# Eight landing places, smaller retrieval parts in front, and half blocks and a third lane in the mixer

## What is computed

```python
def peer_ffn(x, wq, sub_keys, u, v):
    ...
    def chunk(xc):
        q = (xc @ wq).reshape(PEER_CHUNK, PEER_HEADS, 2, half)
        sc = jnp.einsum('chpd,hpnd->chpn', q, sub_keys, preferred_element_type=jnp.float32)
        s1, i1 = lax.top_k(sc[:, :, 0], PEER_TOPK)
        s2, i2 = lax.top_k(sc[:, :, 1], PEER_TOPK)
        ...
        top_s, pos = lax.top_k(cand, PEER_TOPK)
        eidx = jnp.take_along_axis(cidx, pos, axis=-1)
        g = jax.nn.softmax(top_s, axis=-1)
        u_sel = jnp.take(u, eidx, axis=0)
        a = jax.nn.gelu(jnp.einsum('chkd,cd->chk', u_sel, xc, ...), approximate=False)
        w = (g * a).astype(x.dtype)
        v_sel = jnp.take(v, eidx, axis=0)
        return jnp.einsum('chk,chkd->cd', w, v_sel)
...
def second_block(x, c, ctx, c_ctx, w_mod, ...):
        sh1, sc1, g1, sh2, sc2, g2 = [m[:, None, :] for m in _modulation(c, w_mod[i], b_mod[i], 6)]
        cm = _modulation(c_ctx, w_mod[i], b_mod[i], 2 if last else 6)
        hc = _rmsnorm(ctx, norm_mix_pre[i]) * (1.0 + cm[1]) + cm[0]
        sf_c = _state_features(hc, w_in[i], gdn_conv[i], gdn_a_log[i], gdn_dt_bias[i])
        init = _recurrent_mixers(sf_c, None, None, zero_state, ret_log_decay[i])
        ...
        ret_x, gdn_x, _ = _recurrent_mixers(sf_x, _apply_rope(rq, cos, sin), gq, init, ret_log_decay[i])
        x = x + g1 * _rmsnorm(_mixer_out(ret_x, gdn_x, rg, gz, gates, *out_p), norm_mix_post[i])
        h2 = _rmsnorm(x, norm_ffn_pre[i]) * (1.0 + sc2) + sh2
        x = x + g2 * _rmsnorm(_moe(h2, *moe_p), norm_ffn_post[i])
```

## Time and profile before

| | us |
|---|---|
| median of 3 runs (lowest to highest) | 3165.72 (3165.24 to 3170.95) |
| the profiled execution | 3162.61 |
| its span | 3160.8 |
| up to the first gather of layer 0 | 225.5 |
| layer 0, first gather to last sum | 831.9 |
| attention and front of layer 1 | 209.6 |
| layer 1, first gather to last sum | 707.9 |
| mixer, to 2527 | 552 |
| experts, 2527 to the end | 633.8 |

### The profile page before, as it was taken

One profiled execution on the slowest core, in us unless ns is written; L12 is line 12 of the kernel. 1 busy time (PEld: TensorE's weight loads), 2 busy tenths in 40 slices (PEclk: granted clock), 3 DMA queues, 4 the chain that ended last, 5 costly groups with the idle time before them and its releaser, 6 DMA issues.

```text
span 3160.8 us, 29029 instructions
## 1 busy us (share of the span) xinstructions
PE 2464.3 (78%) x9500; PEld 1296.6 (41%) x9500; DVE 1600.1 (51%) x3286; ACT 842.7 (27%) x2277; POOL 830.3 (26%) x718
## 2 busy tenths in 40 slices
PE   7898778878979889888877777868787667667673
PEld 4683334424545467433322222546553432222221
DVE  5554737679777555564758544364533422111112
ACT  1312343443433131233333333322110211111110
POOL 1002323335545210333434433012100012122221
PEclk9799988998989989999999999889998778888786
DMA  6039988897979702999999999210113199999992
GB/s 261 1 125 411 369 345 309 329 385 270 379 285 382 299 27 81 377 412 411 420 421 402 421 421 381 107 40 32 49 54 150 46 408 395 396 384 390 375 380 79
DMA packets 128913, 885.91 MB, mean 280 GB/s; under 512 B 23024, under 2 KB 23408, under 8 KB 31600
## 3 DMA queue, kind: packets, MB, share of 16 engines
q0 software_dynamic: 86976, 553.74, 44.5%
q1 hardware_dynamic: 41776, 330.22, 26.0%
HBM read 877.56 MB, written 37.75 MB: 290 GB/s over the span
## 4 chain that ended last, share of the span: by engine, by line
PE 44%; DMA 24%; DVE 19%; ACT 6%; issue 4%; POOL 2%; SPq 1%; DVEq 0%; POOLq 0%; ACTq 0%
PE ps L155 42%; DMA ring<-in_peer_uv,idx_u 10%; DMA ring<-in_w_gu 5%; DVE ring L1278 5%; ACT arena L125 4%; DVE arena L76 4%; DMA ring<-in_w_down 3%; DMA arena<-in_w_gu 2%; PE ps L158 2%; DVE ring L76 1%; DMA arena<-in_peer_uv,idx_u 1%; DVE iu L113 1%; DVE arena L1278 1%; ACT L125 1%; DVE arena L109 1%
## 5 line engine op out<-in xcount | busy, mean ns | idle before, releaser
L155 PE MATMUL ps<-ring,arena 128*128 128x512 f32 (+3 forms) x3200 | 1234.0, 647 | 305.0 <-ACT arena L125 182.2
L155 PEld LDWEIGHTS ps<-ring,arena 128*128 128x128 f32 (+2 forms) x3200 | 457.9, 180 | 980.8 <-issue 593.7
L1278 DVE CUSTOM_DVE_ANT_0 ring<-ring,h 128x1024 f32<-128x1024 f32 x428 | 538.9, 1259 | 396.0 <-DMA ring<-in_peer_uv,idx_u 368.2
L2335 POOL DMA_INDIRECT ring<-in_peer_uv,idx_u x428 | 466.0, 1089 | 794.2 <-PE ps L155 662.2
L155 PE MATMUL ps<-arena 128*128 128x128 f32 (+7 forms) x2184 | 501.2, 417 | 156.4 <-ACT arena L125 88.6
L125 ACT ACTIVATE arena<-arena 128x1 f32<-128x1 f32 (+3 forms) x1089 | 291.7, 268 | 840.3 <-DVE arena L1278 751.2
L155 PEld LDWEIGHTS ps<-arena 128*128 128x128 f32 (+3 forms) x2184 | 286.2, 197 | 334.4 <-issue 151.1
L155 PE MATMUL ps<-ring,hT 128*128 128x512 f32 (+1 forms) x704 | 323.1, 615 | 44.7 <-DMA ring<-in_w_in 13.1
L76 DVE TENSOR_TENSOR arena<-arena,ps 128x512 f32<-128x512 f32 (+1 forms) x134 | 77.1, 576 | 445.0 <-ACT arena L125 352.9
L125 ACT ACTIVATE arena<-ps 128x512 f32<-128x512 f32 (+5 forms) x182 | 100.3, 551 | 745.6 <-PE ps L155 671.2
L125 ACT ACTIVATE arena<-cst,arena 128x128 f32<-128x128 f32 x512 | 205.5, 401 | 175.1 <-PE ps L155 135.3
(11 more groups left out here) (117 smaller groups left out, 1633.2 us busy)
## 6 DMA issues: line engine op xcount, KB each, us to landing
ring<-in_w_gu SPq DMA_DIRECT2D x98, 1024.0 KB, 29.4
ring<-in_w_down SPq DMA_DIRECT2D x52, 1024.0 KB, 28.1
ring<-in_w_in SPq DMA_DIRECT2D x22, 2048.0 KB, 9.4
arena<-in_w_gu SPq DMA_DIRECT2D x30, 1024.0 KB, 30.4
ring<-in_w_mod SPq DMA_DIRECT2D x12, 2048.0 KB, 11.2
ring<-in_peer_wq SPq DMA_DIRECT2D x8, 2048.0 KB, 7.9
ring<-in_w_o SPq DMA_DIRECT2D x6, 2048.0 KB, 15.9
arena<-in_w_down SPq DMA_DIRECT2D x12, 1024.0 KB, 25.0
```

Source lines behind the costliest of these rows:

```text
L155: return self.e.matmul(o, lhsT, rhs, start=start, stop=stop, skip_group_check=True)
L1278: v.done(v.e.tensor_tensor_reduce(out=row, in0=row, in1=h[:, n // 128, :], scale=1.0, scalar=0.0, op0=ALU.mult, op1=ALU.add, accum_out=aa[ ...
L2335: g.e.indirect_dma_start(out=landing(n), out_offset=None, in_=d["peer_uv"], in_offset=bass.IndirectOffsetOnAxis(ap=idx_u[:, n:n + 1], axis ...
```

## The change

1. **Landing places.** Eight in place of six, in the order (4, 5, 0, 1, 2, 3, 6, 7) for the first gathers; places 6 and 7 are ring areas 0 to 3. The keys move to areas 14 and 15, and the rows of ln2, which were loaded there early, are loaded after the keys' last use.
2. **Units of retrieval.** Five in place of four: 32 rows (heads 0 and 1), 32, 64, 64, 64. Ahead of the sums PE computes queries 0, 1 and 3 of both blocks and the scores of the first two units; queries 2 and the six other scores are computed in pieces behind sums 0 to 13 (`late`). The routes' pieces stand at n = 1 to 22, 25 to 55, 66 to 106 and 130 to 170.
3. **Background.** 131 phases in layer 0 in place of 80, at every second n from 14 and more densely from 193; the context's lanes one after the other, in one set of tiles; w_mod and the context's blocks in the one place at area 16, each loaded after the use of the one before. Layer 1: 18 phases, every fifth n from 14. x's block Rk is no longer loaded ahead of the last gather.
4. **Mixer.** Gq in a third lane; gates in twelve blocks of 256 columns, both c in one bank, in two places (areas 13 and 15), at fixed phases; the zero fill behind the features; one more phase in the norm; w_o2's two blocks in the other order.

Here is PE at the start of the retrieval of layer 0, before. `hT,ring` are queries (64 instructions are two of them), `ring,arena 128x128` scores, `128x512` sums, `small 2x512` the first block of w_mod.

The diff, cut to its core:

```diff
-GATHERS = 6
-SUMS, OTHERS, LATE = ((0, 1), (2, 3)), (4, 5, 6, 7), (4, 5, 6, 7, 0, 1)
+GATHERS = 8
+SUMS, OTHERS = ((0, 1), (2, 3)), (4, 5, 6, 7)
 WQ_AT = (4, 8, 16, 0)
-UNITS = [(0, 0), (0, 1), (1, 0), (1, 1)]
-ROUTE_PIECES, EXP_AT, WEIGHTS_AT = 24, 50, 54
+
+UNITS = [(0, 0, 1, 0), (0, 1, 2, 32), (0, 2, 4, 64), (1, 0, 2, 128), (1, 2, 4, 192)]
+UNIT_OF = [u for u, (c, j0, j1, n0) in enumerate(UNITS) for _ in range(32 * (j1 - j0))]
+
+ROUTE_AT = [[], [n for n in range(1, 23) if n % 3], [n for n in range(25, 56) if n % 3],
+            list(range(66, 108, 2)), list(range(130, 172, 2))]
+EXP_AT, WEIGHTS_AT = (-1, 20, 50, 114, 178), (1, 26, 58, 118, 182)
+LATE_QUERIES = 16
+
+PLACE_OF = (4, 5, 0, 1, 2, 3, 6, 7)
 NORM_AT = (130, 131, 133, 137, 138)
 
 
 def beside(l, n):
 
     if l:
-        return 1 if n in range(4, 104, 10) else 0
-    return 1 if n in range(4, 130, 3) or n in range(138, 252, 3) else 0
+        return 1 if n in range(14, 104, 5) else 0
+    return 1 if n in range(14, 130, 2) or n in range(138, 254, 2) or n in range(193, 249, 4) else 0
...
+GATE_AT = (0, 1, 2, 3, 6, 9, 12, 15, 20, 21, 22, 26)
+GATE_PHASES = 30
...
-        ctx_tiles = [R(i, 1)[:, 512 * j:512 * j + 512] for i in (0, 1, 2, 3, 16, 17, 18, 19) for j in range(2)]
-        ctx_tiles += [ar(14720 + 512 * i, 512) for i in range(9)] + [ar(19328, 512), ar(19840, 512), ar(0, 512)]
-        ctx_lanes = [(ctx_tiles[0:13], ctx_tiles[26]), (ctx_tiles[13:26], ctx_tiles[27])]
+        ctx_tiles = [ar(14720 + 512 * i, 512) for i in range(11)] + [ar(512 * i, 512) for i in (1, 2)]
...
-            i = n % GATHERS
-            return R(4 + 2 * i, 2) if i < 5 else ar(6144, 2048)
+            i = PLACE_OF[n % GATHERS]
+            return R(4 + 2 * i, 2) if i < 5 else ar(6144, 2048) if i == 5 else R(2 * i - 12, 2)
...
+        def gate_place(j):
+            return R(13 + 2 * (j % 2), 2)
+
         def BG(i):
-            return R(0 if i % 2 == 0 else 16, 4)
+            return R(16, 4)
...
+                def late():
+
+                    for c in range(2):
+                        yield from queries(2, c, OTHERS)
+                        for j in (3, 2) if c == 0 else (0, 1, 3, 2):
+                            yield from scores(c, j, OTHERS)
...
-                for hf in range(2):
-                    for c in range(2):
-                        if hf == 0 and c == 0:
-                            turned_rows(0)
-                        queries(2 * hf, c)
-                        queries(2 * hf + 1, c)
-                        if hf == 0 and c == 0:
-                            turned_rows(1)
-                        scores(c, hf)
+                turned_rows(0)
+                run(queries(0, 0))
+                run(queries(1, 0))
+                run(scores(0, 0))
+                turned_rows(1)
+                run(scores(0, 1))
+                for i in (0, 1):
+                    run(queries(i, 1))
+                for c in range(2):
+                    run(queries(3, c))
+                others = late()
...
-                return together(lane(0), lane(1))
+                        yield from gdn_chunk(s, dr, c, ctx_tiles, OTHERS)
+                        yield from ret_chunk(s, dr, c, ctx_kd, None, OTHERS)
+
+                return chain(lane(0), lane(1))
...
+                    conv_features(s, hT, s.conv_blocks2, 1, (4, 5), *ready), gate_columns(s, hT, (6, 7), *ready),
+                    chain(idle(4), conv_features(s, hT, s.conv_blocks3, 2, (6, 7), *ready)), idle(4))
...
+                    for p in range(GATE_PHASES):
+                        for j in gates_at(p):
+                            b = fresh("gate", j, among=(7,))
+                            pe.wait_ge(*at("loaded", "gate", j))
+                            for c in range(2):
+                                for k in range(8):
+                                    t = pe.mm(b[:, c * 256:(c + 1) * 256], hT[:, k, c * P:(c + 1) * P],
+                                              gate_place(j)[:, k * 256:(k + 1) * 256], k == 0, k == 7)
+                            pe.done(t, ("ps", "gate", j), ("used", "gate", j))
+                        yield
...
-                for i, area in ((0, 7), (1, 0)):
+                for i, area in ((1, 0), (0, 7)):
...
                     else:
-                        g.wait_ge(*at("used", "wq", l, i // 2) if i < 4 else at("used", "keys", l))
+                        g.wait_ge(*at("used", "wq", l, i // 2) if i < 4 else at("used", "w_o", l, 0) if i < 6 else
+                                  at("used", "wq", l, 3))
                     g.e.indirect_dma_start(
...
-                    block(0 if i % 2 == 0 else 16, 4, d["w_mod"][i], ("loaded", "w_mod", i),
-                          after=[("used", "w_mod", i - 2) if i - blocks[0] > 1 else before[i % 2]])
+                    block(16, 4, d["w_mod"][i], ("loaded", "w_mod", i),
+                          after=[("used", "w_mod", i - 1) if i > blocks[0] else before])
...
-                block(12, 2, d["peer_keys"][l], ("loaded", "keys", l), after=[("used", "w_o", l, 0)])
-                row(14, 5 + 5 * l, ("loaded", "ln2", l, 0))
-                row(15, 6 + 5 * l, ("loaded", "ln2", l, 1))
+                block(14, 2, d["peer_keys"][l], ("loaded", "keys", l), after=[("used", "w_o", l, 0)])
                 block(16, 4, d["peer_wq"][l, 2], ("loaded", "wq", l, 2), after=[("used", "w_o", l, 1)])
                 block(0, 4, d["peer_wq"][l, 3], ("loaded", "wq", l, 3), after=[("used", "gn", l), ("used", "ln1", l)])
-                before = [("used", "wq", l, 3), ("used", "wq", l, 2)]
+                before = ("used", "wq", l, 2)
+                row(14, 5 + 5 * l, ("loaded", "ln2", l, 0), after=[("used", "keys", l)])
+                row(15, 6 + 5 * l, ("loaded", "ln2", l, 1))
                 if l == 0:
                     load(ctx_rows, rows_of(d["ctx"]), s_ctx, ("loaded", "ctx"), after=[("out", "s", 0, 1, 3)])
                     modulate(range(0, 4), before)
-                    ctx_block(0, "Rk", ("used", "w_mod", 2))
-                    ctx_block(1, "Rv", ("used", "w_mod", 3))
-                    ctx_block(2, "Gk", ("used", "ctx", "Rk"))
-                    ctx_block(3, "Gv", ("used", "ctx", "Rv"))
+                    ctx_block(0, "Rk", ("used", "w_mod", 3))
+                    ctx_block(1, "Rv", ("used", "ctx", "Rk"))
+                    ctx_block(2, "Gk", ("used", "ctx", "Rv"))
+                    ctx_block(3, "Gv", ("used", "ctx", "Gk"))
                 else:
                     modulate(range(4, 12), before)
-            block(0, 4, d["w_in2"][0], ("loaded", "x", "Rk"), after=[("used", "w_mod", 10)])
             block(16, 4, d["w_in2"][4], ("loaded", "x", "Rq"), after=[("used", "w_mod", 11)])
-            block(4, 4, d["w_in2"][2], ("loaded", "x", "Gk"), after=[("used", "gather", 1, 255)])
+            block(0, 4, d["w_in2"][0], ("loaded", "x", "Rk"), after=[("used", "gather", 1, 255)])
+            block(4, 4, d["w_in2"][2], ("loaded", "x", "Gk"), after=[])
...
-            for i, b in enumerate((5, 7, 8, 9, 10, 11)):
-                block(13, 4, d["w_in2"][b], ("loaded", "gate", i),
-                      after=[("used", "gate", i - 1)] if i else [("used", "x", "Rv"), ("used", "x", "Rq")])
-            block(13, 4, d["w_gdn_out"], ("loaded", "merge", 1), after=[("used", "gate", 5)])
+            for j in range(12):
+                block(13 + 2 * (j % 2), 2, d["w_gates"][j], ("loaded", "gate", j),
+                      after=[("used", "gate", j - 2)] if j > 1 else [("used", "x", "Rv"), ("used", "x", "Rq")])
```

346 lines of the change are left out of this document (176 added, 170 removed).

## The result

The changed kernel takes 3095.0 us (median of 4 runs, 3092.4 to 3097.7) against 3166.0 before: a ratio of 0.9773, with a 95% interval of 0.9756 to 0.9789. It is 71 us faster, where 175 were forecast, and lies above the range. Its profiled execution has a span of 3091.6 us, 69.2 less than before.

| | before | forecast of the change | after |
|---|---|---|---|
| first gather of layer 0 | 225.5 | 206.9 | 209.0 |
| layer 0, first gather to last sum | 831.9 | 747 | 824.3 |
| of that, first part / second part | 423.0 / 408.9 | | 413.7 / 410.6 |
| last sum to first gather of layer 1 | 209.6 | 191 | 192.9 |
| layer 1, first gather to last sum | 707.9 | 698 | 721.6 |

A forecast was written before the change was run, and what follows sets the result against it. Layer 0's retrieval was taken as bound by a landing place's round trip, layer 1's by transfers. Gains of 103 (layer 0), 29 (layer 1) and 40 (second block) sum to 172, from 3162.6 to 2991 us; range 2938 to 3072.

The forecast's parts named there:

- The front: Ahead of each layer's sums: less query, score and route work brings the first gather 18.6 us earlier.
- The second block: Conv lanes, mixer gates, w_o2 order, zero fill and norm together gain 40 us, bounds 20 and 58.
- The gates: Mixer: twelve half blocks in two places load one ahead, removing PE's waits; gain 22 us, bounds 8 and 32.
- the third lane: Second block: Gq weights in a third conv lane beside the others save 11 of 12.2 us, bounds 4 and 14.
- w_mod's first block: Layer 0: PE waits some 14 us for its load behind the rows and ctx; costs 9, bounds 3 and 14.
- Layer 0: First retrieval stage: last sum at 954 instead of 1057.4, 103 us gained including the front, bounds 70 and 135.
- DVE 20: Layer 0: expected loss from DVE's dots, routes and background exceeding a transfer per row, 20 us, bounds 8 and 32.
- PE 16: Layer 0, n = 193 to 252: PE needs 2.79 us a row, loss 16 us, bounds 6 and 35.
- Rival (a): DVE or PE becomes layer 0's bound through chained lanes; about 95 us gained, 3067; chance 0.24 together with (d).
- Rival (d): Depth bought but not used, layer 0's losses mostly longer than 9 us; about 85 gained, 3078; 0.24 with (a).
- Rival (c): Slower: more gathers in flight land slower each, 3195 at 0.40 us added; 0.05 with any other slower way.
- The signs: Expected: first gather at 207, layer 0 DMA share 0.97 or more, one 14 us w_mod wait, no gate waits above 2.

The follow-up runs named there:

- the first experiment: Changed kernel with the first block of w_mod of either layer loaded ahead of the ln2 rows and ctx: 3065.4 us, ratio 0.968.
- the combined run: Changed kernel with w_mod's block first, POOL phases behind gather m+7, DVE/ACT ahead from n = 138, 72 phases spread evenly, two conv lanes, new w_o2 order: 3039.8 us.
- the table: Layer 0's 130 phases at rows spaced by PE cost, on the changed kernel with w_mod's block first: 3077.0 us; with DVE/ACT ahead and POOL at m+7 too: 3057.8.
- DVE and ACT ahead: Changed kernel with w_mod's block first, DVE's dots two rows and ACT's weights one row ahead of their background phases: 3067.2 us, ratio 0.9691.
- lag 7: Changed kernel with POOL's background phase of row m behind gather m+7 instead of m+5: 3095.2 us; with w_mod's block first as well 3063.2.
- section 7: Changed kernel with w_mod's block first and no phases beside rows 138 to 255 of layer 0, the 72 left run alone behind the last sum: 3259.1 us.

## Why the prediction was wrong

*The front* was right within 2 us: 18.6 forecast, 16.5 and 16.7 measured. The late queries cost about what was said: from gather 0 to gather 16 it takes 45.0 us in the changed kernel, and 16 x 2.49 are 39.8.

*The second block* was right in its sum, 40 forecast and 42.1 measured, but not in its parts. The gates gave 29.3 instead of 22 (270.8 to 241.5 us), norm, merge and output product behind them 13.7 instead of 8, and the third lane nothing instead of 11; the experts' stage took 1 more. That the sum came out is luck. The third lane was priced by the waits that it would remove, and not by what the same DVE has to do in the meantime for the other lanes. Undoing it gives 6 us.

*w_mod's first block.* The step named the queue, the place and the wait, and sized it at 14 us on PE and 9 on the time, bounds 3 and 14. It was 18.4 and, by the first experiment, 13.7. The same step was left out for layer 1, where the rows stand in the same place of the queue: 15.8 us more. With it, layer 1 is 13.7 us slower from first gather to last sum rather than 10 faster; without it, it would be 2 faster.

*Layer 0* is where the forecast failed: 84 us inside the stage, and 7.6 came, or 21.3 without w_mod's stall. The first part gives 23.5 of these and the second takes 2. The first reading, that the round trip of a landing place bounds the stage, fits the kernel before: in the first part the two places are worth 27 us in the changed kernel too, and in the second the seventh is worth 19.5 beside a schedule of the lanes like the old one.

The step that failed is the price of the new background, which took the chained lanes at no price: for DVE "Spread over 131 phases, one in two rows, that is 0.55 per row", and for PE "2.79 a row" in n = 193 to 252. I counted work, 144 us of DVE and 177 of PE, and work did stay nearly the same. But with w_mod's stall gone rows 138 to 192 take 2.90 us each and rows 193 to 251 take 3.24, where without phases they take 2.48 and 2.50. That is 67 us for the 72 phases, and 68 in the whole part (411.0 against 343.0). Of the terms "DVE 20", "PE 16" and the rest only about 25 fall into that part; 84 are lost there over 128 transfers and the ends (411 - 319 - 8). The places were to take the rest of the old loss, and in this part they had nothing to take: with six of them the new schedule has the same 411 us, 50.6 of DVE's wait for PE and 12.9 of its wait for data.

Why the new schedule is dear is my reading, and isn't shown. There are 72 steps in a row instead of 38 behind n = 138, every one or two rows instead of every three, and DVE takes up PE's product of the phase before ahead of its next dot; with three rows between steps the product is long there, with one or two it isn't. "DVE 20" and "PE 16" compared each engine's work with the transfers, one engine at a time. In the second part DVE has 324 and PE 347 us of work in 411, each with room to spare, and yet 14.1 us more of DVE's work add 15.3, and 23.9 more of PE's add 8.5.

PE's work was also read too low: 1.78 us for a sum comes from sums in a row, while one that stands alone takes 1.98. And 2.79 less 2.49 is 0.30 a row, so that term was 18 by its own numbers and not 16. `beside` has 130 phases, not 131. The bounds of layer 0 and of the second block are narrower than the lows and highs of their terms add up to (10 to 59 for the second block, where 20 to 58 is given).

*The rivals.* Rival (a), "DVE or PE becomes layer 0's bound", named the chained lanes and "a round trip on PE rather than hiding behind the other lane", and gave 3067; the kernel without w_mod's stall takes 3065. Its loss of 120 us in layer 0 is met (810.6 less the floor of 690), and the stall came on top. That the total agrees is in part luck: it had 25 us from layer 1 and 30 from the second block, where 18 and 42 came. A lane's step also got hardly dearer: 68 us for 72 steps are 0.94 each, and 66 (408.9 less 343.0) for 38 pairs of steps before are 0.87, an estimate that takes 343.0 for both. Rival (d), depth that isn't used, holds for the second part, but not for its reason, incidents longer than 9 us. Rival (c) is refuted: with eight gathers under way they are still 2.48 to 2.49 us apart. By the Trainium skill, "SBUF — State Buffer", under "SBUF: two separate sides", DVE and GpSimd can hold a pair of ports against each other; dots of 2.28 and 2.05 us stand beside POOL's multiplies in the changed kernel as well, but the number of the multiplies is the same before and after, and so is the mean dot from a ring place, 1.29 us. No run here isolates their share.

*The signs.* The first gather came at 209.0 instead of 207, PE's one wait on w_mod was 18.4 us, and no gate wait is above 2 us. Layer 0's DMA share is 0.88 instead of 0.97 or more. Rows 193 to 251 are "2.8 us or more", but at 3.24 far more than was priced. PE's waits for ACT in the second part rose from 33 to 50, which isn't one for each of the 72 phases: the sign set for this failure was on another wait than the one that grew, DVE's for PE.

*What stays open*: which part of the new schedule, the chained order, the dense rows or the four banks, leaves the places nothing to do; chained lanes with all 72 phases at even rows and nothing else changed weren't run. Also open is how the 68 us of the lanes divide between DVE's own steps and its waits for PE, and why the even rows gave less in the combined run than the table did. The best second part, 376 us, needed DVE and ACT ahead, lag 7 and the table at once, and its first part was 430. A version with seven places, lanes side by side and DVE ahead wasn't tried.

## What to carry to other kernels

Memory for a deeper buffer comes from somewhere: before counting what the depth brings, look at what the work that gave up its room now does in a row instead of side by side. Run the new order with the old depth as well: its waits tell whether anything is left for the depth to take. When steps of two engines alternate inside a loop, work and busy share alone don't show the slack; add a known amount to each engine and see how much of it comes out. And where a queue of loads is reordered, look for every place where the same loop body runs, and load first what is needed first.

## What the runs showed of the hardware

Gathers of 1 MB keep their 2.49 us with eight under way instead of six (1924.79 to 1927.28 in layer 1, where POOL waits for a place each time). Nothing else of it was unexpected: in the bare lanes of section 7 the granted clock falls to 0.65 of full speed, with PE busy for 151 of 258 us in short products.
